# The 32 matrix states of the sample streams: only read in their loop, renewed from a second load inside the second feed-forward

## The reference, cut to what matters

```python
num = einsum('bqsh,bshd->bqhd', sc, vc) + a[..., None] * einsum('bqhk,bhvk->bqhv', qc, C)   # C is read
...
C_new = decay[..., None, None] * C + einsum('blh,blhv,blhk->bhvk', wg, vc, kc)              # C is renewed
```

```python
def conv_ffn(x, buf, w_up, conv_w, conv_b, w_down):
    u = x @ w_up                                   # 1024 -> 5632
    uc, new_buf = causal_dwconv(u, buf, conv_w, conv_b)
    gate, val = uc[..., :D_FF], uc[..., D_FF:]
    return (gelu(gate) * val) @ w_down, new_buf    # 2816 -> 1024
```

## Time and profile before

| | |
|---|---|
| median of 3 runs | 3905.59 us (3903.67 to 3906.49) |
| profiled execution, span from first to last instruction | 3903.4 us |
| TensorE busy | 3481.6 us, 89% |
| VectorE, ScalarE, GpSimd busy | 49%, 29%, 13% |
| second feed-forward, from its first to its last product | about 3001 to 3836 us |
| loop over the states, with its barriers | 1969.9 to 2220.9 us |

### The profile page before, as it was taken

One profiled execution on the slowest core, in us unless ns is written; L12 is line 12 of the kernel. 1 busy time (PEld: TensorE's weight loads), 2 busy tenths in 40 slices (PEclk: granted clock), 3 DMA queues, 4 the chain that ended last, 5 costly groups with the idle time before them and its releaser, 6 DMA issues. The chain is left out here.

```text
span 3903.4 us, 53745 instructions
## 1 busy us (share of the span) xinstructions
PE 3481.6 (89%) x20489; PEld 3262.9 (84%) x20489; DVE 1908.1 (49%) x2953; ACT 1149.8 (29%) x1880; POOL 511.1 (13%) x769
## 2 busy tenths in 40 slices
PE   5549989999999989999478779997995999999997
PEld 4449989999999989999344468887985999999996
DVE  8933554445444563222533346664655544454455
ACT  5233343332333232222222212222112323323321
POOL 2240111000000120000120032221001100000000
PEclk8679999999999999999678789998997999999998
DMA  3444431111111123332399632222122111111112
GB/s 78 140 121 137 134 96 44 39 44 44 39 44 44 57 101 120 106 104 94 84 262 297 214 92 81 75 67 76 38 71 75 44 39 44 44 41 42 44 38 101
DMA packets 366303, 337.08 MB, mean 86 GB/s; under 512 B 42888, under 2 KB 294024, under 8 KB 365956
## 3 DMA queue, kind: packets, MB, share of 16 engines
q1 hardware_dynamic: 345318, 288.49, 24.1%
q0 software_dynamic: 13600, 38.24, 3.7%
q10 hardware_dynamic: 7176, 7.35, 0.6%
HBM read 231.12 MB, written 100.53 MB: 85 GB/s over the span
## 5 line engine op out<-in xcount | busy, mean ns | idle before, releaser
L1583 PE MATMUL pair<-x_head,w_head 128*128 128x384 f32 x1488 | 505.6, 340 | 53.0 <-DVE w_rest L840 30.4
L1583 PE MATMUL pair<-x_rest,w_head 128*128 128x384 f32 x1488 | 502.5, 338 | 0.0
L1583 PE MATMUL pair<-x_head,w_rest 128*128 128x384 f32 x1488 | 502.1, 337 | 0.0
L840 DVE TENSOR_TENSOR w_rest<-w_raw,w_head 128x1024 fp32r<-128x1024 f32 x228 | 291.9, 1281 | 414.4 <-ACT w_head L836 414.3
L836 ACT ACTIVATE w_head<-w_raw 128x1024 fp32r<-128x1024 f32 x228 | 242.4, 1063 | 686.8 <-PE pair L856 166.9
L1238 PE MATMUL pair<-x_head,w_head 128*128 128x384 f32 x1056 | 354.0, 335 | 10.5 <-DVE w_rest L840 7.5
L1238 PE MATMUL pair<-x_rest,w_head 128*128 128x384 f32 x1056 | 353.5, 335 | 0.0
L1238 PE MATMUL pair<-x_head,w_rest 128*128 128x384 f32 x1056 | 353.5, 335 | 0.0
L1583 PEld LDWEIGHTS pair<-x_head,w_head 128*128 128x128 f32 x1488 | 283.5, 191 | 58.0 <-issue 52.5
L1328 DVE SCALAR_TENSOR_TENSOR cv<-u,par,cv 128x1024 f32<-128x1024 f32 x88 | 112.8, 1282 | 358.5 <-ACT u L1294 358.5
L1583 PEld LDWEIGHTS pair<-x_rest,w_head 128*128 128x128 f32 x1488 | 283.5, 191 | 0.0
(11 more groups left out here) (510 smaller groups left out, 6982.0 us busy)
## 6 DMA issues: line engine op xcount, KB each, us to landing
w_raw<-in_ffn_w_up_dram SPq DMA_DIRECT2D x88, 512.0 KB, 3.9
hs<-in_state_mlstm_C_dram SPq DMA_DIRECT2D x52, 512.0 KB, 6.6
out_dram<-hs SPq DMA_DIRECT2D x52, 512.0 KB, 4.5
w_raw<-in_s_w_glu_dram SPq DMA_DIRECT2D x48, 512.0 KB, 4.1
w_raw<-in_ffn_w_down_dram SPq DMA_DIRECT2D x44, 512.0 KB, 3.7
w_raw<-in_mlstm_w_up_dram SPq DMA_DIRECT2D x32, 512.0 KB, 4.3
xm_d<-xm SPq DMA_DIRECT2D x16, 576.0 KB, 3.9
xc_d<-xc SPq DMA_DIRECT2D x16, 576.0 KB, 2.8
```

Of the source, the lines that this page charges most:

```text
L840: dve.tensor_tensor(self.rest[slot][:, :], self.raw[slot][:, :], self.head[slot][:, :].bitcast(F32), ALU.subtract).then_inc(self.split, 1)
L1583: m = pe.matmul(out[:, 0:TB], lhs[slot][:, P * k:P * k + P], rhs[:, k, TB * c:TB * c + TB], start=(k == 0 and q == 0), stop=(k == KD - 1 a ...
```

## The change

- The loop's block of `mlstm_streams` only loads, turns and reads the states. Four rooms instead of five; one load of 1 MB per state, with rows in the order (p, r, t) so that a partition gets rows that lie side by side. ScalarE copies turned banks 0 and 2, VectorE 1 and 3. There are four sets of turned states, and after each fourth state `meet` issues the reads of four streams, which use the four column strips, one after another for each k.
- A room is free as soon as its state is turned. No stores, no update products, no VectorE updates and no stack loads are left there.
- The first block writes each part straight to where a stack of 48 rows needs it (`vk_d`: six writes per head instead of four), and keeps the 32 decays in SBUF (`decay`). Some operands are read or written with a stride of four to match the new row order.
- `ffn` gets a class `Renewal`. Each state is renewed in two halves of 128 x 1024; 64 halves are spread over the "ticks", one after each up tile and one after down tiles 3 and 7, four in block 0 and six in each later one. At a tick TensorE makes two products of 48 rows by 128 x 512 into banks 6 and 7 (once the half before has been renewed), VectorE makes one scalar_tensor_tensor over 1024 elements per partition, and SP, behind the tick's weight load, stores the half renewed four ticks earlier in its own count, loads the parts, and loads the next half.

Its core:

```diff
+class Renewal:
+    def __init__(self, env, C_in, c_out, vk_d, decay):
...
+        self.room = [env.sb(f"c_room{k}", [P, 2, DH]) for k in range(2)]
+        self.vk = env.sb("vk", [P, 2, DH], F32R)
...
+        self.sums = env.pair[3]
...
+    def load_parts(self, sp, b, p, n):
...
+        sp.dma_start(self.vk[self.row(p, n), :, :].bitcast(F32).rearrange("p m d -> p (m d)"), src).then_inc(self.mark(n), 16)
+    def load(self, sp, b, n):
+        if not isinstance(b, int) or 6 * b + n - 2 >= 2:
+            sp.wait_ge(self.stored[n % 2], self.unit(b, n) * 16)
+        sp.dma_start(self.room[n % 2][:, :, :], self.rows_of(self.old, b, n)).then_inc(self.old_in[n % 2], 16)
+    def store(self, sp, b, n):
+        sp.wait_ge(self.renewed, self.half(b, n) + 1)
+        sp.dma_start(self.rows_of(self.new, b, n), self.room[n % 2][:, :, :]).then_inc(self.stored[n % 2], 16)
+    def sync(self, sp, b, p, n):
+        if self.inside(b, n - 4):
+            self.store(sp, b, n - 4)
+        if n % 2 and self.inside(b, n - 1):
+            self.load_parts(sp, b, p, n - 1)
+        if self.inside(b, n - 3):
+            self.load(sp, b, n - 3)
+    def tensor(self, pe, b, p, n):
+        if not isinstance(b, int) or 6 * b + n - 2 > 0:
+            pe.wait_ge(self.renewed, self.half(b, n))
+        pe.wait_ge(self.mark(n), (b + ((n // 2 - 1) // self.MARKS + 1)) * 16)
+        for q in range(2):
+            t, row = 2 * (n % 2) + q, self.row(p, n)
+            m = pe.matmul(self.sums[:, DH * q:DH * q + DH], self.vk[row, 0, P * t:P * t + P], self.vk[row, 1, :], start=True, stop=True)
+        m.then_inc(self.grown, 1)
+    def vector(self, dve, b, n):
...
+        dve.wait_ge(self.old_in[n % 2], (u + 1) * 16)
+        dve.wait_ge(self.grown, self.half(b, n) + 1)
+        dve.scalar_tensor_tensor(out=room[:, :, :], in0=room[:, :, :], scalar=by, in1=self.sums[:, :].rearrange("p (t k) -> p t k", t=2),
+                                 op0=ALU.mult, op1=ALU.add).then_inc(self.renewed, 1)
...
 (ffn, SP)      w.load(sp, n + k, k % 2, src, first=isinstance(n, int) and n + k < 2)
+               renewal.sync(sp, b, p_, tick(b, k))
 (ffn, TensorE) m.then_inc(upped if c < NB - 1 else w.used, 1)
+               renewal.tensor(pe, b, par_, tick(b, k))
+               if m % 4 == 3 and ups is not None:
+                   renewal.tensor(pe, ups, 1 - s, 4 + m // 4)
 (ffn, VectorE) w.subtract(dve, n + (k + 2), k % 2)
+               renewal.vector(dve, b, tick(b, k))
                if k == 3 and not start:
                    adds(b - 1, n + 4, True, 0, 2)
...
                if m % 4 == 3 and more:
                    w.subtract(dve, n + (2 + m // 4), m // 4)
+                   renewal.vector(dve, b + 1, 4 + m // 4)
...
 (mlstm_streams, first block)
-                    for dst, src in ((v_parts[h, 0], v_head), (v_parts[h, 1], v_rest), (k_parts[h, 0], k_head), (k_parts[h, 1], k_rest)):
-                        sp.dma_start(dst, src[h % 2]).then_inc(wrote[h % 2], 16)
+                    for m, parts in enumerate(((v_head, v_head, v_rest), (k_head, k_rest, k_head))):
+                        for j, part in enumerate(parts):
+                            sp.dma_start(vk_d[:, h, j, :, m, :], part[h % 2]).then_inc(wrote[h % 2], 16)
...
 (the loop)
+                for n in range(ROOMS, SR):
+                    sp.wait_ge(turned, HT * (n - ROOMS + 1))
+                    c_load(sp, n)
...
+                def meet(q):
+                    h, r = order[QUAD * q]
+                    for k in range(HT):
+                        pe.wait_ge(by_act if k % 2 == 0 else by_dve, 2 * QUAD * q + 2 * (QUAD - 1) + k // 2 + 1)
+                        for pair in range(QUAD):
+                            ins = pe.matmul(bank[4 + 2 * (h % 2)][32 * pair:32 * pair + 32, :],
+                                            qz[h][k][:, 64 * pair + 32 * r:64 * pair + 32 * r + 32],
+                                            cts[pair][k], start=False, stop=(k == HT - 1), skip_group_check=True)
+                    ins.then_inc(inter, 1)
...
                     for k in range(HT):
-                        over(pe, copied, HT * i - HT + k + 1)
+                        over(pe, by_act if k % 2 == 0 else by_dve, 2 * i - 2 + k // 2 + 1)
                         for t in range(HT):
                             ins = pe.transpose(bank[k][:, P * t:P * t + P], craw[b][t][:, P * k:P * k + P], env.ident[:, :])
                         ins.then_inc(turned, 1)
-                    if i % 2 == 0:
-                        updates()
...
+                    if i % QUAD == QUAD - 1:
+                        meet(i // QUAD)
...
 (VectorE)
-                        dve.scalar_tensor_tensor(out=room[t], in0=room[t],
...
+                    for k in (1, 3):
+                        dve.wait_ge(turned, HT * i + k + 1)
+                        if k == 1:
+                            over(dve, inter, i // QUAD)
+                        dve.tensor_copy(cts[i % SETS][k], bank[k][:, :]).then_inc(by_dve, 1)
```

More of the change, by code:

```diff
@@ L1149, in ffn @@
+def ffn(env, w_up, w_down, par, tails, x_head, x_rest, f, states):
     nc, w, banks = env.nc, env.w, [env.bank[0:NB], env.bank[NB:2 * NB]]
@@ L1162, in ffn @@
         gelued, acted, headed, rested = (env.sem(n) for n in ("gelued", "acted", "headed", "rested"))
+        renewal = Renewal(env, *states)
+        tick = lambda b, k: k + 2 if isinstance(b, int) and b == 0 else k
         come, upped, down, added, tap = env.sem("come"), env.sem("upped"), env.sem("down"), env.sem("added"), env.sem("tap")
@@ L1199, in downs @@
                         w.load(sp, n + h, h, rows[:, :, 4 * P * h:4 * P * h + 4 * P])
+                        renewal.sync(sp, b + 1, 1 - p_, first + h)
                 blocks(sp, body)
-                downs(FBLOCKS - 1, last)
+                downs(FBLOCKS - 1, (FBLOCKS - 1) % 2, last, 0)
+                for n in (2, 3):
+                    renewal.sync(sp, FBLOCKS, FBLOCKS % 2, n)
+                renewal.ended(sp)
             @block.gpsimd
@@ L3106, in _ @@
-                for p in range(ROOMS):
-                    sp.wait_ge(c_kept[p], (32 if p < ROOMS - 1 else 64) * ((SR - 1 - p) // ROOMS + 1))
+                for n in range(ROOMS, SR):
+                    sp.wait_ge(turned, HT * (n - ROOMS + 1))
+                    c_load(sp, n)
+                for k in range(2):
+                    sp.wait_ge(wrote[k], 2 * PARTS_OUT)
             @block.tensor
             def _(pe):
-                def reads(i, k):
-                    h, s = order[i]
-                    pair, r = s // 2, s % 2
-                    pe.wait_ge(copied, HT * i + k + 1)
-                    return pe.matmul(bank[4 + 2 * (h % 2)][32 * pair:32 * pair + 32, :], qz[h][k][:, 64 * pair + 32 * r:64 * pair + 32 * r + 32],
-                                     cts[i % 2][k], start=False, stop=(k == HT - 1), skip_group_check=True)
@@ L3118, in _ @@
-                for i, (h, s) in enumerate(order):
-                    pair, r = s // 2, s % 2
-                    def updates():
-                        for t in range(HT):
-                            over(pe, updated, HT * i + t - 1)
-                            row = slice(64 * r, 64 * r + S3)
-                            pe.matmul(bank[5 + 2 * (t % 2)][:, :], v3[h % 2][row, pair, P * t:P * t + P],
-                                      k3[h % 2][row, pair, :], start=True, stop=True).then_inc(added, 1)
+                def meet(q):
[7 more added lines that the diff above has]
+                    ins.then_inc(inter, 1)
@@ L3138, in _ @@
                         ins.then_inc(turned, 1)
-                    if i % 2 == 0:
-                        updates()
-                    else:
-                        for k in range(HT):
-                            for j in (i - 1, i):
-                                ins = reads(j, k)
-                        ins.then_inc(inter, 1)
-                        updates()
+                    if i % QUAD == QUAD - 1:
+                        meet(i // QUAD)
             @block.scalar
@@ L3504, in program @@
         env.new_phase()
+        own.close()
         env.scope, env.units = passed, 0
```

166 lines of the change are left out of this document (81 added, 85 removed).

## The result

The changed kernel takes 3816.26 us, median of 4 runs (3814.13 to 3819.85), against 3905.49 us (3903.67 to 3906.49) for the one before on the same chip: ratio 0.9772 (0.9760 to 0.9785). The forecast was 3817, so the sum was right. Two of its terms were not: each is some 9 us off, and by luck they cancel.

The account below looks back on a forecast made before the run. TensorE and the transfers together were taken to bound the loop, TensorE the second feed-forward. Saving 143 us and adding 54 gave -89, from the 3905.6 us median to 3817; 8-in-10 range 3786 to 3866.

Parts of the forecast that it names:

- The loop: Loop over the 32 sample states: new phase 109 us (106 + 3) in place of 251.
- fewer pauses speak for the better one; I take 103: Loop's clock: between 110 us at clock 0.82 and 101 at 0.90, it took 103 for TensorE.
- The entry: First block up to the loop: start 1.3 us sooner, strided operands left at nothing, some 10 us at double time.
- the loop starts some 1.3 us sooner: Before the loop: last writes go from four to six DMAs, but six load issues become one; start before 1969.87.
- The insertions: Second feed-forward: each pair of 48-row products costs TensorE 0.75 us with its changes of shape, 64 of them 48 us.
- VectorE's stall: Second feed-forward, row sums: VectorE 1.28 us later, TensorE 0.75, so a new stall of 0.53, in ten blocks 5 us.
- 1 (two strips only, or a low clock): Loop: four strips go only two at a time, or clock stays mostly at half; time 3846, chance 0.2.
- 2 (late loads): Second feed-forward: states' loads land late behind weight loads and stores, VectorE and TensorE wait; 30 us, 3847, chance 0.15.
- 3 (the clock in the feed-forward): Second feed-forward: insertions let TensorE's clock fall, 64 of them cost 109 us; time 3926, chance 0.04.
- 4: Whole kernel: the stores moved out of the loop simply are the cost elsewhere; time near 3900, chance 0.03.

Follow-up runs that it names:

- the other two changes: Old row order without strides, and the first block's six part writes issued by GpSimd; with the padding, against the kernel before: 3796.16 us, ratio 0.9715.
- the third experiment: Changed kernel with the renewal's TensorE products left out, VectorE's operation reading the room from SBUF instead of the banks: 3772.03 us, ratio 0.9663.

## Why the prediction was right, and where it was not

**The loop, 9 us better than summed.** Predicted 109, measured 99.9. By term: transposes 57.3 us (512 at 0.112 from 7.17/64) where I had 63.0, since 1.97/16 counts the last one's tail each time; reads 27.5 as predicted (8 x 8 x 0.43); ends 3.4, with the first product, for 3; loads late 2.4 (2.03 and smaller) for 3. I left out the other three products with `v`: four heads, four products, of which three lie inside the loop, 1.87 each, 5.6 us. What outweighs them is the clock: I took 11.6 us for a mixed clock, from a stage that paused up to 5 us for its stores, and the granted clock was 0.97; what remains in the sum for it and for the changes to and from the reads (0.8 predicted) is 3.7. The step "fewer pauses speak for the better one; I take 103" had the direction right and the size wrong: with the pauses gone the clock went nearly to full.

**The entry, 9 us worse.** The step that failed is "the loop starts some 1.3 us sooner". It counted DMA requests by their number, at the 0.4 to 0.5 us each of the kernel before, and left the strides at nothing with 10 us as the bound. The first block came out at +7.5: 5.4 us from three periods of 10.25 for 8.4 on average (1933.78 to 1959.10 before, 1932.99 to 1963.75 after), 0.7 inside the last head, and 1.4 from SP's tail, where six scattered writes and one load take 6.9 us (1969.74 to 1976.67) and four writes and six loads took 5.5. The bound was wide enough; the choice in it was the wrong end. The other kernels with this block took 52.8 to 55.8 us, so the loss against the one trace of before is 5 to 8 us. The 0.5 us of one strided copy is not what costs most: it lengthens a pause of TensorE by 0.7 us, and behind the longer pause the next 32 products took 1.6 us more, in every head instead of one in three. That this period comes from the strides and not from the queue, the two runs with only one of them taken away show; that the clock is the link is read from the 32 heads above, not tried by itself. Why the same kernel without strides is then held by late inputs and late writes is shown as waits, not taken apart: whether it is the number of writes, their scattered rows or their bytes was not tried.

**The insertions, right in sum and in cause.** 0.75 us were predicted and 0.75 measured, at a clock of 1.00; the run without a change of shape takes away the part put down to it. Of the three intervals only the first came as read: 0.27 for 0.26. The two products are 0.335 apart where I took 0.23 from durations in the earlier trace rows (the starts of such a pair are 0.338 apart there too), and the next full one follows 0.323 later where I took 0.43; these two errors of 0.1 cancel, by luck. One part was missing: 0.11 us on the next gap, 7.0 us in all.

**VectorE's stall, wrong.** Predicted 5 us more; TensorE's waits for `f` fell from 3.4 us (up and down tiles, 5 waits) to 2.2 (1.5 and 0.7, 10 waits). I set 1.28 against one insertion of 0.75. Before down tile 4 there are two insertions, since the one after down tile 3 delays TensorE there as well: 1.72 against VectorE's 1.28, and the old stall at that place goes; a small one of 0.2 comes before down tile 2. With 48.2 + 7.0 for the insertions, 1.2 less for the waits and some 2 less at the jumps of the hardware loop, where an insertion lies in a gap that was there before, the stage comes to 52.0 for the measured 52.3: this error and the missing 0.11 cancel by luck, too. Without TensorE's part the stall is the 10.6 us of the third experiment.

**The rivals.** 1 (two strips only, or a low clock): no; four reads share 0.43 us, and the clock is 0.97. 2 (late loads): none of VectorE's waits is for `c_room`; a half lands 5.7 us after its issue. 3 (the clock in the feed-forward): 1.00 throughout. 4: the stores cost nothing where they now are.

**Better than both.** 48 rows padded to 128 give 3797.4 us, and with the other two changes 3796.2; the intervals of their ratios overlap, so the padding is all that can be told: 16 to 19 us, nearly 0.5% of the changed kernel, of which 15 are in the feed-forward.

## What to carry to other kernels

Work moved from a stage bound by transfers and waits to one bound by TensorE costs there exactly its time between the starts of the neighbours, so read that price from a trace: for small products the change of shape was nearly half of it, and padding to the neighbours' shape bought more than half of that back. Delays on two engines don't add: the shorter hides in the longer, and taking one away brings the other out. And where TensorE's granted clock falls after its pauses, half a microsecond more on another engine can come with four times that on TensorE.

## What the runs showed of the hardware

- Reads of 128 x 32 by 128 x 512, fp32, in four column strips begin together every 0.43 us, as two do; the reads of a second pair of strips, issued behind those of the first, began before these had ended (12 rounds where one pair after the other would be 16).
- Two products of 48 rows between full ones of 128 x 384: 0.86 us. With 128 rows, 0.46.
- Operands with a stride of four elements: ScalarE's copy of 128 x 512 takes 1.14 us for 0.63, two product records 2.05 for 1.12.
- After a pause of TensorE of 1.76 us its next 32 products took 3.8 us in 8 heads of 11 (kernel before, and without strides) and 5.3 to 5.4 in the other 3; after 2.48 us they took 5.3 to 5.4 in all 21.
- The end of a block came 7.9 and 8.0 us after GpSimd's last DMA issue, in a drain of GpSimd of 9.1 us, and 0.7 us after SP's.
- A write of 256 KB in scattered rows of 2 KB held SP for 0.6 to 2.45 us; the same bytes in order, mostly 0.45.

```profile
1963.15 2.45 SPq L3060 DMA_DIRECT2D vk_d<-f  x1
```
